# Squared MLP blocks: transposed by VectorE in squares and moved by DMA, instead of transposed by TensorE

## The reference

```python
    u = _rmsnorm(h, norm_mlp_g[layer])
    a = jnp.einsum('bsd,df->bsf', u, w_up[layer])      # 2048 -> 8192
    a = jnp.square(jax.nn.relu(a))
    h = h + jnp.einsum('bsf,fd->bsd', a, w_down[layer])
```

## Time and profile before

| | us |
|---|---|
| median of 3 runs | 2296.09 (2295.31 to 2297.19) |
| the profiled execution | 2295.4 |
| its span | 2293.6 |

### The profile page before, as it was taken

The page is one execution under the profiler, slowest core; times in us unless marked ns, Lnnn a source line. Parts: engine busy times, 40 slices in busy tenths (PEclk is TensorE's granted clock), DMA queues, the critical chain, the costliest instruction groups (busy, mean ns, idle before and its releaser), DMA issues.

```text
span 2293.6 us, 28901 instructions
## 1 busy us (share of the span) xinstructions
PE 2274.0 (99%) x10409; PEld 1871.3 (82%) x10409; DVE 1545.7 (67%) x1837; ACT 1107.3 (48%) x1515; POOL 160.8 (7%) x233
## 2 busy tenths in 40 slices
PE   9999999999999999999999999999999999999998
PEld 7888888888888888888878877787888888888886
DVE  7886778778867777886767664556445544555546
ACT  6445555555544545545563454544444344444444
POOL 0121001111111111110011000000000000000000
PEclk9999999999999999999999999999999999999999
DMA  8982679978888888886677664655555656555553
GB/s 310 330 271 96 210 237 317 324 261 290 279 284 279 272 297 274 270 280 209 233 231 253 202 200 128 208 188 172 195 184 188 216 185 197 187 190 195 187 181 127
DMA packets 245908, 523.92 MB, mean 228 GB/s; under 512 B 20096, under 2 KB 20496, under 8 KB 244496
## 3 DMA queue, kind: packets, MB, share of 16 engines
q1 hardware_dynamic: 214256, 405.32, 54.1%
q0 software_dynamic: 29568, 111.97, 14.0%
q10 hardware_dynamic: 1952, 4.85, 0.6%
HBM read 517.87 MB, written 4.21 MB: 228 GB/s over the span
## 4 chain that ended last, share of the span: by engine, by line
PE 96%; DVE 1%; DMA 1%; ACT 1%; issue 1%; SPq 0%; DVEq 0%; POOLq 0%; ACTq 0%
PE acc L1750 29%; PE acc L1759 29%; PE acc L1754 29%; PE tp L1821 2%; DMA mring<-w_mod 1%; PE m L1832 1%; PE acc L1772 0%; PE acc L1777 0%; DVE macc L1091 0%; PE acc L1782 0%; PE tp L2158 0%; DVE wlo L1061 0%; PE tp L2176 0%; PE tp L2170 0%; PE acc L1952 0%
## 5 line engine op out<-in xcount | busy, mean ns | idle before, releaser
L1061 DVE TENSOR_TENSOR wlo<-wring,whi 128x1024 fp32r<-128x1024 f32 x762 | 919.8, 1216 | 583.1 <-ACT whi L547 474.0
L547 ACT ACTIVATE whi<-wring 128x1024 fp32r<-128x1024 f32 (+1 forms) x510 | 532.0, 1047 | 729.7 <-PE acc L1759 728.5
L1750 PE MATMUL acc<-whi,xhi 128*128 128x512 f32 x2056 | 559.4, 394 | 0.1
L1754 PE MATMUL acc<-whi,xlo 128*128 128x512 f32 x2056 | 550.2, 389 | 0.0
L1759 PE MATMUL acc<-wlo,xhi 128*128 128x512 f32 x2056 | 550.0, 389 | 0.0
L1754 PEld LDWEIGHTS acc<-whi,xlo 128*128 128x128 f32 x2056 | 386.0, 188 | 81.2
L1759 PEld LDWEIGHTS acc<-wlo,xhi 128*128 128x128 f32 x2056 | 386.0, 188 | 80.7
L1750 PEld LDWEIGHTS acc<-whi,xhi 128*128 128x128 f32 x2056 | 380.7, 188 | 85.6 <-issue 9.0
L557 ACT ACTIVATE whi<-wring 128x1024 fp32r<-128x1024 f32 x266 | 280.6, 1059 | 319.6 <-PE acc L1759 317.9
L1091 DVE SCALAR_TENSOR_TENSOR macc<-mring,csil,macc 128x512 f32<-128x512 f32 x480 | 344.0, 746 | 29.2 <-DMA mring<-w_mod 23.1
L450 POOL DMA_DIRECT2D mring<-w_mod x192 | 138.8, 723 | 1048.2 <-DVE macc L1091 999.9
(11 more groups left out here) (273 smaller groups left out, 1252.2 us busy)
## 6 DMA issues: line engine op xcount, KB each, us to landing
wring<-w_up SPq DMA_DIRECT2D x216, 512.0 KB, 4.7
wring<-w_down SPq DMA_DIRECT2D x216, 512.0 KB, 5.2
mring<-w_mod POOLq DMA_DIRECT2D x192, 512.0 KB, 5.2
wring<-w_in SPq DMA_DIRECT2D x184, 512.0 KB, 5.0
wring<-w_gate SPq DMA_DIRECT2D x88, 512.0 KB, 4.2
wring<-w_out SPq DMA_DIRECT2D x64, 512.0 KB, 4.8
gbig<-ctx_in POOLq DMA_DIRECT2D x2, 1024.0 KB, 9.3
hspill<-h ACTq DMA_DIRECT2D x1, 2048.0 KB, 9.1
```

Of the source, the lines that this page charges most:

```text
L547: act.activation(whi[:, piece_slot(c, piece), 0:half], wring[:, g4, piece * half:(piece + 1) * half], ACT.Copy).then_inc(hi_done, 1)
L1061: dve.tensor_tensor(wlo[:, h4, 0:half], wring[:, g4, piece * half:(piece + 1) * half], whi[:, h4, 0:half].bitcast(F32), ALU.subtract).then ...
L1750: pe.matmul(acc[:, 2 * pair + t, :], hi[:, tile, t * P:(t + 1) * P], whi[:, h4, w], start=(tile == starts), stop=False)
L1754: pe.matmul(acc[:, 2 * pair + t, :], lo[:, tile, t * P:(t + 1) * P], whi[:, h4, w], start=False, stop=False)
```

## The change

Of the four squared blocks of a chunk, three (blocks 0, 1 and 2) are no longer transposed by TensorE. VectorE transposes each in squares of 32x32 (`turn_squares`, two instructions of 128x512, after groups 5, 9 and 13), writing into `blk2`. A 128x128 transpose is then complete but for the place of the squares: square (i, j) must go to (j, i), across partitions. ScalarE starts 16 transfers for that, each of 32 partitions by 256 columns (32 KB), from `blk2` to `tmpT` (`move_squares`, after groups 6, 10 and 14). After groups 7, 11 and 15 it waits until all have landed and rounds four tiles into `xhi` (`round_squares`), and VectorE takes four remainders into `xlo` (`remain_squares`). Block 3 goes as before. TensorE waits, ahead of group 16, for all twelve remainders of the chunk. The counts of PSUM banks are adapted.

```diff
+        turned = blk2[:, :, :].rearrange("p a n -> p (a n)").rearrange("p (j k t b) -> p t k j b", j=4, k=KG, t=T)
+        strips = blk2[:, :, :].rearrange("p a n -> p (a n)").rearrange("p (j n) -> p j n", j=4)
+        placed = tmpT[:, :, :].rearrange("p a n -> p (a n)").rearrange("p (i n) -> p i n", i=4)
+        moved = tmpT[:, :, :].rearrange("p a n -> p (a n)").rearrange("p (i k t b) -> p k t i b", i=4, k=KG, t=T)
...
+                if j:
+                    act.wait_ge(relu_turned, c.at("rt", 0, T))
...
+            def move_squares():
+
+                c.add("rt")
+                act.wait_ge(relu_turned, c.at("rt", 0, T))
+                if c.n["rt"] > 1:
+                    act.wait_ge(relu_lo, c.at("rt", -KG, KG))
+                for j in range(4):
+                    for i in range(4):
+                        act.dma_start(placed[32 * j:32 * j + 32, i, :], strips[32 * i:32 * i + 32, j, :]).then_inc(relu_moved, 16)
+
+            def round_squares(tile):
+
+                act.wait_ge(relu_moved, c.at("rt", 0, MOVES))
+                for k in range(KG):
+                    act.activation(xhi[:, tile + k, :].rearrange("p (t i b) -> p t i b", t=T, i=4),
+                                   moved[:, k], ACT.Copy).then_inc(relu_hi, 1)
 
...
-                    if 1 <= j <= 4:
+                    if j == 4:
                         round_banks(xhi, 4 * (j - 1), 2)
                     round_group(4 * j + 2)
+                    if 1 <= j <= 3:
+                        move_squares()
                     round_group(4 * j + 3)
+                    if 1 <= j <= 3:
+                        round_squares(4 * (j - 1))
...
+            def turn_squares(j):
+
+                dve.wait_ge(blk_ready, c.at("rblk", j))
+                for t in range(T):
+                    dve.transpose(turned[:, t], blk[:, t, :].rearrange("p (k j b) -> p k j b", k=KG, j=4)).then_inc(relu_turned, 1)
+
+            def remain_squares(tile):
+
+                for k in range(KG):
+                    c.add("rh")
+                    dve.wait_ge(relu_hi, c.at("rh"))
+                    dve.tensor_tensor(xlo[:, tile + k, :].rearrange("p (t i b) -> p t i b", t=T, i=4), moved[:, k],
+                                      xhi[:, tile + k, :].bitcast(F32).rearrange("p (t i b) -> p t i b", t=T, i=4),
+                                      ALU.subtract).then_inc(relu_lo, 1)
...
-                    if g % 4 == 1 and 1 <= j <= 4:
+                    if g % 4 == 1 and 1 <= j <= 3:
+                        turn_squares(j)
+                    elif g % 4 == 3 and 1 <= j <= 3:
+                        remain_squares(4 * (j - 1))
+                    elif g == 17:
...
+                    if j == 4:
+                        pe.wait_ge(relu_lo, c.at("rt", 3 * KG, KG))
...
-                        if kg == 1 and 1 <= j <= 4:
+                        if kg == 1 and j == 4:
```

More of the change, by code:

```diff
@@ L246, in two_blocks @@
         mg_in = sem("mg_in")
+        relu_turned, relu_moved, relu_hi, relu_lo = (
+            sem(n) for n in ("relu_turned", "relu_moved", "relu_hi", "relu_lo"))
         out_s = sem("out_s")
@@ L358, in two_blocks @@
         BANKS = {"z": 1, "suffix": 1, "ctx_state": 1, "state": 2, "turn": 1, "out": 1, "conv": 2}
[L360 removed]
+        T_O = 8 + 8 + 2 * MLP_CHUNKS + 8 + 8 + 4 + BANKS["out"] + sum(
             BANKS.get(step[0], 0) for steps in BESIDE[1].values() for step in steps)
         H_MLP = H0 + 4 + 4 * MLP_CHUNKS
+        MOVES = 16 * 16
         block = ctx.enter_context(nc.Block())
@@ L848, in _ @@
             root_and_scale(2, u_g, u_g)
-            with c.loop(act, MLP_CHUNKS - 1, 1, g=32, q=8, half=4, blk=4, ha=4, ssq=4 * T, mt=5):
+            with c.loop(act, MLP_CHUNKS - 1, 1, g=32, q=2, half=4, blk=4, ha=4, ssq=4 * T, mt=5, rt=3):
                 mlp_chunk()
@@ L2045, in mlp_chunk @@
                 c.add("blk", 4)
+                c.add("rt", 3)
             mlp_chunk(True)
-            with c.loop(pe, MLP_CHUNKS - 1, 1, g=32, q=8, ma=80, ha=4, half=4, blk=4):
+            with c.loop(pe, MLP_CHUNKS - 1, 1, g=32, q=2, ma=80, ha=4, half=4, blk=4, rt=3):
                 mlp_chunk()
```

6 lines of the change are left out of this document (3 added, 3 removed).

## The result

| | before | after |
|---|---|---|
| median of 3 runs, us | 2296.09 | 2396.33 (2394.39 to 2397.33) |
| ratio of after to before, 95% interval | | 1.0432 (1.0417 to 1.0446) |
| the profiled execution, span, us | 2295.4, 2293.6 | 2394.39, 2392.7 |

The direction was right and the size three times too small: +100 us where the prediction said +33, and outside its range of 2308 to 2365.

The account below looks back on a forecast made before the run. TensorE was taken as the bound. Per chunk, 9.1 us of stalls plus 1.8 of clock less 2.65 removed gave +8.2, +33 over four chunks on 2295.4; forecast 2329.5 us, range 2308 to 2365.

Parts of the forecast that it names:

- What bounds the kernel: Whole kernel: TensorE, busy 99% of the span; other engines count only when they make it wait.
- 12 x 0.88 = 10.6 us removed: TensorE's transposes of three blocks in each of four chunks, all on the path: 10.6 us saved.
- VectorE turns, 0.6 us each: VectorE turns each block in two instructions of 128x512: 0.6 us each, 1.2 us a block.
- The roundings: ScalarE rounds four tiles of 128x256 of moved squares per block: 1.4 us.
- ScalarE issues 16 transfers, 0.42 us each: ScalarE's row of issues per block: 6.7 us for 16, no weight rounding meanwhile; ends 0.37 and 0.6 us each.
- my first rival: ScalarE bounds everywhere: issues of 0.5 us or landings of 5.2 us, all three blocks late; 2344 to 2370, chance 0.25.
- The last transfer lands after 3.0 us: Landing of each block's last 32 KB transfer, before ScalarE rounds the squares: 3.0 us, ends 2.4 and 5.2.
- The walk: One chunk followed from TensorE's end of group 6: stalls of 9.1 us, 8.6 at the boundary of groups 15 and 16.
- The wait at the sums: After group 15, TensorE waits 5.3 us for VectorE's last modulation step before transposing the sums.
- The clock, 1.8 us a chunk: Behind the waits around group 16, TensorE runs some 3.6 us at half rate: 1.8 us lost per chunk.
- The second: Rival: issues of 0.3 us or a short landing, VectorE doesn't fall behind; +5.5 us a chunk, 2318, chance 0.12.
- The third: Rival: issues don't hold ScalarE, TensorE waits only 3.0 us a chunk, clock doesn't fall; 2297.5, chance 0.04.

Follow-up runs that it names:

- pe_alone: Changed kernel without turning, moving, rounding and remainders of the three blocks and without TensorE's wait for them, so only what is removed: 2285.27 us.
- the probes: Kernel before with rows of transfers added behind its last work, nothing else moving: 0.64 us an issue between SBUF ends, 0.46 to 0.48 with HBM at one end.
- four: Changed kernel with only 4 of the 16 transfers of each block, all waits, roundings and remainders kept: 2315.43 us.
- no_moves_late: Changed kernel without the transfers, and groups 16, 17 and 18 each waiting only for their own block's remainders: 2290.06 us.
- keep_clock: Changed kernel with TensorE filling most of its two long waits, at the sums and before group 16, with matmuls nobody reads: 2394.52 us.
- block1: Kernel before with only block 1 turned by VectorE and moved through HBM, blocks 0, 2 and 3 by TensorE: 2296.64 us.
- no_moves: Changed kernel without the transfers and the wait for their landing; turn, rounding, remainders and waits among engines stay: 2309.62 us.
- late_wait: Complete changed kernel, but groups 16, 17 and 18 each wait only for their own block's remainders: 2376.06 us.

## Why the prediction was wrong, step by step

**What bounds the kernel, and 12 x 0.88 = 10.6 us removed.** Right (pe_alone: -11.8, with 10.6 inside its interval).

**VectorE turns, 0.6 us each.** 0.686 in the mean, 1.30 for the pair. Near enough; the estimate from the Trainium skill ("VectorE: DVE Perf Modes", "The three transpose paths"), 1.24 us, worked out from a figure for one bf16 tile, doesn't hold for this fp32 form. The roundings (1.34 for four) and remainders (1.42 to 1.54) were right too.

**ScalarE issues 16 transfers, 0.42 us each.** The first step that failed: 0.64 with the gap, 10.1 to 11.9 us a row instead of 6.7. My upper end, 0.6, was taken from other transfers, and rows 7 hold none with both ends in SBUF; the probes show that this pair of ends costs 0.64, where one end in HBM costs 0.46. It's beyond the condition of my first rival (0.5), which had the right mechanism: all three blocks late, stalls ahead of groups 9 and 13. With few issues (four) these stalls are gone.

**The last transfer lands after 3.0 us.** The second step that failed: 5.4 in the median, 6.32 for the last one of the third block in chunk 1. My upper end (5.2) was nearly right, my choice was not: I took the small quiet transfer of the earlier trace rows as the nearest, and the load beside it, 84% of the DMA engines' time, went into no term. In the quiet the same transfer takes 1.9 us.

**The walk.** With t = 0 at 565.25 us in chunk 1 (0.2 us ahead of ScalarE's first rounding behind group 6), the third block's issues were to start at 47.6, end at 54.4, and the last remainder be there at 59.2. They ran from 57.2 to 67.4, and the remainder was there at 75.1: 3.4 us more for the issues, 2.9 for landing, rounding and remainders, and 9.6 from the blocks before. So before group 16 the wait was 8.5, not 3.3, and for weight pieces, mostly ahead of groups 9 and 13, 6.9 us a chunk (27.6 in all), not 0.5. The wait at the sums was 4.9 against 5.3 predicted: right, and for the reason given, VectorE held by ScalarE and with no room to catch up (both ends of the wait came some 9.5 us later than walked). 36 us of waits were predicted, 82.5 came. The last remainder came 15.9 us late in chunk 1, and four times that is 64 of the 67 us by which the forecast missed: the path was the right one, and two terms on it were too small.

**The clock, 1.8 us a chunk.** Behind the wait before group 16 it was 2.1 us: right. TensorE's busy time lost 6.6 us a chunk, since the stalls ahead of groups 9 and 13 and at the sums have their own slow stretches behind them, and I hadn't foreseen those. By the chain they cost nothing, since TensorE wasn't on the path there. That they cost nothing is luck, for I hadn't asked where the path lies.

**The rivals.** The first (ScalarE the bound everywhere, 2344 to 2370, at 0.25) was the truth, with both of its conditions exceeded; it should have had the greater chance, since a row of the trace stood for each. Its way of pricing holds too: 16 x 0.22 us for the issues and 2.4 us for the landing are 5.9 us more a block, which by the estimate of three late blocks in each of four chunks gives 2400, and 2396 was measured. The second rests on cheap issues; the sentence of the Trainium skill ("DMA: Bandwidth & Descriptors", "Issuing engines are not separate DMA queues") that a start is usually small beside the transfer is true of one start here, 0.61 us beside a landing of 5.4, but the sum is what counts: the starts follow one another and the landings overlap, so 16 starts took 10.4 us and the landing of the last 5.4 more. The third was mispriced: without any transfer it is 2310, not 2297.5, for a wait of 2.5 us lowers the clock as well. A gain would have been there at zero transfer cost with the wait in its right place (no_moves_late, 2290), which I hadn't seen, and the prediction's sentence that only much faster VectorE operations could bring a gain is wrong: the diff has one wait for three blocks, and I took it as given rather than ask which group needs which block.

**What stays open.** Whether a run with the clock held in all four chunks behind group 16's wait would give back the 8.4 us that the chain puts on it (keep_clock was too weak), and where block1's missing 3.5 us are.

## What to carry to other kernels

Price a row of small transfers by its issues on the engine that starts them, with the issue time of the same pair of ends, and the landing by the load beside it; if the trace has neither, the range must hold both at their slow ends together. A chain that hangs from an engine with 8% of slack (here VectorE, 5.0 us in 5.44) passes every delay on to the next deadline. Before costing a wait, ask of each waiting step which part of the data it needs: here a wait per block was worth 20 us. And before costing a slow clock, ask whether the engine is on the path there: here 18 of 26.5 us of slower matmuls weren't.

## What the runs showed of the hardware

- An issue from SBUF to SBUF holds its sequencer for 0.61 us (0.64 with the gap), on ScalarE's queue and on SyncE's (0.59), in 32x256, 128x64 and 128x256 alike; to or from HBM it is 0.44, and 0.34 for a single one.
- A transfer of 32 KB from SBUF to SBUF lands after 1.9 us when nothing else moves and after 5.4 (2.7 to 6.9) beside weight loads.
- VectorE's STREAM_TRANSPOSE of 128x512 fp32 takes 0.686 us, two in a row 1.30.
- Idle times of 2.5 us (no_moves and four, before group 16, all eight chunks, with 0.8 to 3.5 us idle at the sums just ahead) put TensorE at its 1.2 GHz level, and the next groups took 1.4 to 3.0 us longer. The length of a gap alone doesn't tell: 1.93 us (after, ahead of group 9 of chunk 1) and 1.91 (keep_clock) did it too, while 2.02, 2.27 and 2.94 (keep_clock) and 3.29 (late_wait, at the sums of chunk 0) left the clock at 1.00.
